# First attention in pairs of heads: suffix sums later, and from a high and a low part

## The chip, the cores and the metric

One core of a Trainium2 chip runs the whole program. Five engines work side by side, each through its own instructions in order: TensorE (PE: matmuls, and the loads of their stationary operand, PEld), VectorE (DVE), ScalarE (ACT), GpSimd (POOL), and SyncE (SP), whose queue issues the DMAs. They meet only at semaphores. The metric is the device time of the program in microseconds, the median of several runs.

## The reference, cut to what matters

The program computes one transformer block of one kind and then two of another, for 256 positions and a width of 1024, in float32. The change lies in the first block, in its "stick-breaking" attention (8 heads of 64 columns, queries in blocks of 128 positions):

```
z = q.k / sqrt(64)                                    for every query t and key s
log_not = where(s < t, log_sigmoid(-z), 0)
suffix = cumsum(log_not, over s, reverse) - log_not   # sum over the keys after s
a = where(s < t, exp(log_sigmoid(z) + suffix), 0)
o = a @ v                                             per head
```

Beside it the block computes `gates = sigmoid(h @ w_in[:, the last 3 * 1024 columns])`; the outputs of the attention, of a pooling branch and of a gating branch go through matrices of their own, are multiplied by these gates, and are added.

## The kernel before, in words

**Weights come in units.** Every large weight matrix is streamed from HBM in 153 units of 1 MB (128 partitions x 2048 numbers) through a ring of 4 slots (`raw`, `hi`, `lo`). float32 products are made from parts that TensorE takes in one pass: ACT copies a unit to the reduced type fp32r (`hi`, L356), DVE subtracts (`lo = raw - hi`, L367), and PE adds up three products per tile: high by high, low by high, high by low. `unit_x` (L466) does this with the activations as the stationary operand: for each of the two tiles of 128 positions (`for tt`), 4 k-tiles x 3 products of 512 columns, 12 matmuls a tile, 24 a unit. When its last matmul ends it raises `used`, ACT splits the unit that comes four units later (`act_step`), and DVE follows (`dve_step`). So a unit is split some three units ahead of its use, and for the weights alone neither ACT nor DVE has to hurry.

**The stage of the change.** The gates need 12 units, `s = 0..11`. The attention of the 8 heads is woven in between them, so that its chain through ACT and DVE runs beside matmuls of the units. In the code before, step `s` of PE is (block of TensorE, `for s in range(12)`):

- the 24 matmuls of gate unit `s`;
- `scores(s)`: z of head `s` into a PSUM bank, two matmuls (L1510, L1512) that use 64 of the 128 rows of the array;
- `suffix(s - 1)`: three matmuls with the constant matrices `tri` and `ones`, in float32, which add `log_not` up over the later keys;
- `values(s - 2)`: two matmuls with `vS`, which use 64 of the 128 output columns.

A float32 matmul stands in the trace as two instructions (two passes), an fp32r matmul as one.

ACT's step: the split of the unit (L356), `softplus(s)` (Abs, Exp, Ln: L1844, L1846, L1847), the exponential of head `s - 1` (L1881), in odd steps the high part of the attention's output (`o_split`, L1850) and the copy of a finished gate (L1858). DVE's step: the low part of the unit (L367), the argument of head `s - 1` (L2099: it adds the suffix sum from PSUM), `log_not(s)` (five instructions, L2081, L2083, L2087, L2089, L2091; `lnot_done` rises after the third), and in odd steps the low part of the output (L2107). In step 1 DVE also makes the norm of the gating branch (`gating_norm`, from L2060 to L2065). Only PSUM bank 6 holds a suffix sum, so `suffix(h)` waits until the argument of head `h - 1` has been read (`arg_done`).

After the gate units' step 9, PE makes the products of the pooling and the gating branch ("mixing", the 4 and 16 matmuls that read `wpd` and `wsT`), and in unit 10 goes on without attention work.

The order of work is what is written: no scheduler changes it. Each engine stands still at an instruction whose semaphore has not come, and everything behind it on that engine stands too.

## Time and profile before

| | us |
|---|---|
| median of 3 runs | 1027.43 |
| lowest, highest | 1025.7, 1028.62 |
| the profiled execution, its own time | 1026.62 |
| span of its trace | 1024.8 |
| PE busy | 1010.8 (99%) |
| DVE busy | 719.6 (70%) |
| ACT busy | 492.0 (48%) |
| stage of the change (scores of head 0 to gate unit 10) | 71.94 to 146.64 |

The program is one long row of matmuls, and an engine other than PE matters only where PE waits for it. The trace gives for each instruction its start and its duration. Matmuls overlap (a matmul of 512 columns is shown with 0.39 us, but the next starts 0.23 us later), so what a matmul costs is read from start to start; the same holds for ACT and DVE, whose instructions overlap by about 0.1 us.

### The profile page before, as it was taken

Reading aid. Unit: us, or ns where it says so; the run is one execution under the profiler, and the core shown is the slowest. Engines: PE = TensorE matmul, PEld = TensorE weight load, DVE = VectorE, ACT = ScalarE, POOL = GpSimd, SP = SyncE. Lnnn points to the kernel's source line nnn. Section 1 sums busy time; section 2 is a strip of 40 time slices with the busy share of each in tenths; the row PEclk is TensorE's granted clock in tenths of the full one; section 3 lists DMA queues with packets and bytes.
Section 4 is the critical chain, followed back from the end, with each engine's and each line's share of the span. In section 5 each row is a group of like instructions: output and inputs, shape, how many; then the busy total and the mean of one; then the engine's idle time right before and its main releaser. Section 6 shows DMA issues by size and latency. Waiting matters only on the chain.

```text
span 1024.8 us, 16248 instructions
## 1 busy us (share of the span) xinstructions
PE 1010.8 (99%) x6616; PEld 886.9 (87%) x6616; DVE 719.6 (70%) x882; ACT 492.0 (48%) x559; POOL 108.4 (11%) x83
## 2 busy tenths in 40 slices
PE   8999999999999999999999999999999999999998
PEld 8997778899999888986899999988886689999997
DVE  6869657987667787854887767677976776445664
ACT  6455564553444436432554343445556665343431
POOL 1031000000010000225001000010001301000000
PEclk9999999999999999999999999999999999999999
DMA  9984345749788784595639877786461536665641
GB/s 319 368 277 155 129 136 182 286 168 343 258 285 282 277 274 146 170 311 156 224 110 346 284 281 276 254 284 222 171 226 56 171 118 212 199 198 175 201 165 42
DMA packets 120031, 223.77 MB, mean 218 GB/s; under 512 B 6622, under 2 KB 21408, under 8 KB 119968
## 3 DMA queue, kind: packets, MB, share of 16 engines
q1 hardware_dynamic: 117584, 214.97, 61.6%
q0 software_dynamic: 2256, 7.88, 2.4%
q8 instruction: 45, 0.74, 0.3%
q14 instruction: 18, 0.15, 0.0%
q10 hardware_dynamic: 128, 0.03, 0.0%
HBM read 217.17 MB, written 1.05 MB: 213 GB/s over the span
## 4 chain that ended last, share of the span: by engine, by line
PE 88%; DVE 7%; issue 2%; ACT 1%; DMA 1%; POOL 1%; SPq 0%; DVEq 0%; ACTq 0%; POOLq 0%
PE ps L461 84%; DMA ada_raw<-in_ada_w 1%; PE ps L1120 1%; DVE lo L367 1%; PE ps L951 1%; ACT aS L1977 1%; DVE X L922 1%; PE ps L817 1%; POOL aS L2422 1%; DVE stat L2322 1%; PE ps L1510 0%; DMA X<-in_x 0%; DVE y_tmp L921 0%; ACT hi L356 0%; PE ps L1717 0%
## 5 line engine op out<-in xcount | busy, mean ns | idle before, releaser
L367 DVE TENSOR_TENSOR lo<-raw,hi 128x2048 fp32r<-128x2048 f32 x151 | 349.2, 2319 | 221.1 <-ACT hi L356 220.7
L356 ACT ACTIVATE hi<-raw 128x2048 fp32r<-128x2048 f32 x151 | 289.1, 1915 | 303.2 <-PE ps L461 274.8
L461 PE MATMUL ps<-hTh,hi 128*128 128x256 f32 x992 | 265.7, 286 | 1.1 <-DVE lo L367 0.6
L461 PE MATMUL ps<-hTh,lo 128*128 128x256 f32 x992 | 262.4, 283 | 0.0
L461 PE MATMUL ps<-hTl,hi 128*128 128x256 f32 x992 | 261.0, 283 | 0.0
L461 PEld LDWEIGHTS ps<-hTh,hi 128*128 128x128 f32 x992 | 182.1, 192 | 4.0 <-issue 2.8
L461 PEld LDWEIGHTS ps<-hTl,hi 128*128 128x128 f32 x992 | 181.7, 192 | 1.5 <-issue 1.2
L461 PEld LDWEIGHTS ps<-hTh,lo 128*128 128x128 f32 x992 | 182.2, 192 | 0.0
L461 PE MATMUL ps<-hi,hidh 128*128 128x512 f32 (+1 forms) x424 | 164.6, 388 | 0.0
L461 PE MATMUL ps<-hi,hidl 128*128 128x512 f32 (+1 forms) x424 | 163.5, 386 | 0.0
L461 PE MATMUL ps<-lo,hidh 128*128 128x512 f32 (+1 forms) x424 | 163.4, 385 | 0.0
L461 PE MATMUL ps<-hi,hTh 128*128 128x512 f32 (+1 forms) x328 | 128.0, 390 | 0.8 <-DVE hTl L2336 0.2
L461 PE MATMUL ps<-lo,hTh 128*128 128x512 f32 (+1 forms) x328 | 124.5, 380 | 0.0
L461 PE MATMUL ps<-hi,hTl 128*128 128x512 f32 (+1 forms) x328 | 122.0, 380 | 0.0
L1143 DVE SCALAR_TENSOR_TENSOR ada_acc<-ada_raw,cond,ada_acc 128x512 f32<-128x512 f32 x147 | 112.1, 762 | 7.1 <-DMA ada_raw<-in_ada_w 2.5
L1069 POOL TENSOR_TENSOR sqr<-relu 128x1024 f32<-128x1024 f32 x24 | 46.2, 1924 | 478.6 <-ACT relu L1037 478.6
L461 PEld LDWEIGHTS ps<-lo,hidh 128*128 128x128 f32 x424 | 79.6, 188 | 16.1
L461 PEld LDWEIGHTS ps<-hi,hidh 128*128 128x128 f32 x424 | 79.7, 188 | 15.9 <-DVE lo L367 0.5
L461 PEld LDWEIGHTS ps<-hi,hidl 128*128 128x128 f32 x424 | 79.7, 188 | 15.5 <-issue 0.5
L461 PEld LDWEIGHTS ps<-hi,hTh 128*128 128x128 f32 x328 | 61.7, 188 | 16.9 <-issue 3.8
L461 PEld LDWEIGHTS ps<-lo,hTh 128*128 128x128 f32 x328 | 61.7, 188 | 12.0
L461 PEld LDWEIGHTS ps<-hi,hTl 128*128 128x128 f32 x328 | 61.8, 188 | 11.0 <-issue 0.2
(248 smaller groups left out, 857.8 us busy)
## 6 DMA issues: line engine op xcount, KB each, us to landing
raw<-in_mlp_w SPq DMA_DIRECT2D x64, 1024.0 KB, 5.2
ada_raw<-in_ada_w SPq DMA_DIRECT2D x44, 1024.0 KB, 7.5
raw<-in_w_in SPq DMA_DIRECT2D x20, 1024.0 KB, 7.7
raw<-in_w_ff_in SPq DMA_DIRECT2D x16, 1024.0 KB, 5.4
raw<-in_w_ff_out SPq DMA_DIRECT2D x16, 1024.0 KB, 5.3
raw<-in_attn_w_qkv SPq DMA_DIRECT2D x12, 1024.0 KB, 6.1
raw<-in_conv_w_in SPq DMA_DIRECT2D x8, 1024.0 KB, 6.7
taps<-u_pad SPq DMA_DIRECT2D x64, 71.0 KB, 5.5
```

The source lines that it names most:

```text
L356: nc.scalar.activation(hi[:, slot], raw[:, slot], ACT.Copy).then_inc(hi_made, 1)
L367: nc.vector.tensor_tensor(lo[:, slot], raw[:, slot], hi[:, slot].bitcast(F32), ALU.subtract).then_inc(lo_made, 1)
L461: return nc.tensor.matmul(o, lhs, rhs, start=start, stop=False, skip_group_check=True)
L817: nc.tensor.matmul(ps[:, bank, 0:P], ident if by is None else by, ident if by is None else by, start=True, stop=True)
L922: nc.vector.tensor_tensor(x, x, y, ALU.add).then_inc((x_half, x_ver)[c], 1)
L951: nc.tensor.matmul(ps[:, 7], ones, ada_acc[:], start=True, stop=True).then_inc(ada_cols, 1)
L1069: nc.gpsimd.tensor_tensor(sqr[:], relu[:], relu[:], ALU.mult).then_inc(sq_done, 1)
L1120: last = nc.tensor.matmul(ps[:, bank, q:q + 1], acc[:, q * P:(q + 1) * P], ones[:, 0:1], start=True, stop=True)
L1143: ins = nc.vector.scalar_tensor_tensor(out=acc, in0=w, scalar=s, in1=acc, op0=ALU.mult, op1=ALU.add)
L1977: nc.scalar.activation(a, a, ACT.Exp, scale=SCALE, bias=s_col(k, 4 + j, 1), accum_out=s_col(k, 8 + j, 1)).then_inc(s_exp, 1)
L2322: link(dve, nc.vector.tensor_reduce(s_col(s, 2 * j, 2), aS[:, s % 4, :, c], AX.X, ALU.max))
L2422: nc.gpsimd.tensor_tensor(a, a, y, ALU.mult).then_inc(s_p, 1)
```

## The change

Four things change, all in the stage of the gate units:

- **Pairs.** `scores(k)` and `values(k)` now do heads `2k` and `2k+1` together, in even steps only. The two heads' matmuls stand next to each other, those of 256 columns first, then those of 128.
- **Later.** `suffix` of the even head comes at the end of the next, odd unit; `suffix` of the odd head in the middle of the unit after that (a new argument `middle` of `unit_x`, called between its two tiles); then `values(k)` and `scores(k + 1)` at that unit's end.
- **Two passes.** The suffix sum is made from an fp32r high part (`high(h)`, a copy on ACT) and an fp32r low part (a subtraction on DVE, the sixth instruction of `log_not`), with fp32r copies of the constants (`tri_r`, `ones_r`, made once on ACT): six fp32r matmuls instead of three float32 ones. The new semaphores are `hi_kept`, `lnot_lo` and `tri_kept`.
- **Order on ACT and DVE.** In even steps DVE does `log_not` of both heads, and ACT `softplus` of both, then `high` of both. The argument of the even head (`argument(s - 1)` in odd steps) stands behind that step's `dve_step`; the exponential of the even head stands behind `act_step`.

```diff
@@ -173,7 +173,10 @@
         sbt = ada_area("sbt", 4096, [P, 2, 3, 384])
+        sbt_r = ada_area("sbt_r", 4096, [P, 2, 3, 384], F32R)
         gt = ada_area("gt", 4096, [P, 3, 512])
+        tri_r = big("tri_r", 32768, [P, P], F32R)
+        ones_r = row_area("ones_r", 11648, [P, P], F32R)
...
@@ -460,7 +466,8 @@
-        def unit_x(pe, u, j, act_h, act_l, k0, outs, first, nk=4, cols=512, final=False, need=None, tail=None):
+        def unit_x(pe, u, j, act_h, act_l, k0, outs, first, nk=4, cols=512, final=False, need=None, tail=None,
+                   middle=lambda: None):
 
             slot = slot_of(u, j)
             pe.wait_ge(lo_made, u + 1)
@@ -484,6 +491,8 @@
                 return
             parts = UNIT // nk // cols
             for tt in range(TT):
+                if tt:
+                    middle()
                 for c in range(parts):
                     last = products(outs(tt, c), tt, slice(c * cols, (c + 1) * cols), first,
                                     need if tt == 0 and c == 0 else None)
@@ -1500,37 +1509,48 @@
                    True, nk=8, cols=SEQ)
             ada_sum(pe, 1)
 
-            def scores(h):
-                if h == 0:
+            def both(k):
+
+                return [(2 * k + i, slice(HD * i, HD * i + HD)) for i in range(2)]
+
+            def scores(k):
+                if k == 0:
                     pe.wait_ge(qkv_kept, 2)
-                if h >= 2:
-                    pe.wait_ge(arg_done, h - 1)
-                r = slice(HD * (h % 2), HD * (h % 2) + HD)
-                k = h // 2
-                nc.tensor.matmul(ps[:, 4 + h % 2, 0:SEQ], kT[r, k, 0:P], qT[r, k, :], start=True,
-                                 stop=False, skip_group_check=True)
-                nc.tensor.matmul(ps[:, 4 + h % 2, SEQ:384], kT[r, k, P:SEQ], qT[r, k, P:SEQ],
-                                 start=False, stop=False, skip_group_check=True).then_inc(z_done, 1)
+                else:
+                    pe.wait_ge(arg_done, 2 * k)
+                for h, r in both(k):
+                    nc.tensor.matmul(ps[:, 4 + h % 2, 0:SEQ], kT[r, k, 0:P], qT[r, k, :], start=True,
+                                     stop=False, skip_group_check=True)
+                for h, r in both(k):
+                    nc.tensor.matmul(ps[:, 4 + h % 2, SEQ:384], kT[r, k, P:SEQ], qT[r, k, P:SEQ],
+                                     start=False, stop=False, skip_group_check=True).then_inc(z_done, 1)
 
             def suffix(h):
 
-                pe.wait_ge(lnot_done, h + 1)
+                pe.wait_ge(hi_kept, h + 1)
                 if h >= 1:
                     pe.wait_ge(arg_done, h)
-                t = sbt[:, h % 2, 1]
-                mm(pe, ps[:, 6, 0:SEQ], tri, t[:, 0:SEQ], True)
-                mm(pe, ps[:, 6, P:SEQ], ones, t[:, SEQ:384])
-                mm(pe, ps[:, 6, SEQ:384], tri, t[:, SEQ:384]).then_inc(sfx_done, 1)
-
-            def values(h):
-                pe.wait_ge(a_done, h + 1)
-                if h >= 2 and h % 2 == 0:
-                    pe.wait_ge(o_lo, h // 2)
-                a = sbt[:, h % 2, 2]
-                r, at = slice(HD * (h % 2), HD * (h % 2) + HD), (h // 2 % 2) * SEQ
-                v = slice(h * HD, h * HD + HD)
-                mm(pe, ps[r, 7, at:at + SEQ], vS[:, 0, v], a[:, 0:SEQ], True)
-                mm(pe, ps[r, 7, at + P:at + SEQ], vS[:, 1, v], a[:, SEQ:384]).then_inc(av_done, 1)
+                if h == 0:
+                    pe.wait_ge(tri_kept, 2)
+                for i in range(2):
+                    t = sbt_r[:, h % 2, i]
+                    if i:
+                        pe.wait_ge(lnot_lo, h + 1)
+                    mm(pe, ps[:, 6, 0:SEQ], tri_r[:], t[:, 0:SEQ], i == 0)
+                    mm(pe, ps[:, 6, P:SEQ], ones_r[:], t[:, SEQ:384])
+                    last = mm(pe, ps[:, 6, SEQ:384], tri_r[:], t[:, SEQ:384])
+                last.then_inc(sfx_done, 1)
+
+            def values(k):
+                pe.wait_ge(a_done, 2 * k + 2)
+                if k:
+                    pe.wait_ge(o_lo, k)
+                at = (k % 2) * SEQ
+                for h, r in both(k):
+                    mm(pe, ps[r, 7, at:at + SEQ], vS[:, 0, h * HD:h * HD + HD], sbt[:, h % 2, 2, 0:SEQ], True)
+                for h, r in both(k):
+                    mm(pe, ps[r, 7, at + P:at + SEQ], vS[:, 1, h * HD:h * HD + HD],
+                       sbt[:, h % 2, 2, SEQ:384]).then_inc(av_done, 1)
 
             for s in range(12):
                 g = s // 2
@@ -1542,14 +1562,15 @@
                     pe.wait_ge(gelu_done, 2)
                 elif s % 2 == 0:
                     pe.wait_ge(gate_kept, g - 1)
+                odd_head = s % 2 == 0 and 2 <= s <= SB_HEADS
                 unit_x(pe, U_GATE + s, None, hTh, hTl, 4 * (s % 2), lambda tt, c: ps[:, bank + tt],
-                       s % 2 == 0)
-                if s < SB_HEADS:
-                    scores(s)
-                if 1 <= s < SB_HEADS + 1:
+                       s % 2 == 0, middle=(lambda: suffix(s - 1)) if odd_head else lambda: None)
+                if s % 2 and s < SB_HEADS:
                     suffix(s - 1)
-                if 2 <= s < SB_HEADS + 2:
-                    values(s - 2)
+                if odd_head:
+                    values(s // 2 - 1)
+                if s % 2 == 0 and s < SB_HEADS:
+                    scores(s // 2)
                 if s == 9:
 
                     pe.wait_ge(pool_in, 1)
@@ -1833,6 +1854,9 @@
             gelu(ps[:, 2], gv[:].rearrange("p t n -> p (t n)"))
             nc.scalar.preload_act_table_set("natural_log_exp_and_others")
 
+            nc.scalar.activation(tri_r[:], tri, ACT.Copy).then_inc(tri_kept, 1)
+            nc.scalar.activation(ones_r[:], ones, ACT.Copy).then_inc(tri_kept, 1)
+
             def softplus(h):
 
                 act.wait_ge(z_done, h + 1)
@@ -1845,6 +1869,15 @@
                 act.wait_ge(abs_done, h + 1)
                 link_act(act, nc.scalar.activation(t, t, ACT.Exp, scale=-1.0))
                 nc.scalar.activation(t, t, ACT.Ln, bias=1.0).then_inc(soft_done, 1)
+
+            def weights(h):
+                act.wait_ge(arg_done, h + 1)
+                a = sbt[:, h % 2, 2]
+                nc.scalar.activation(a, a, ACT.Exp).then_inc(a_done, 1)
+
+            def high(h):
+                act.wait_ge(lnot_done, h + 1)
+                nc.scalar.activation(sbt_r[:, h % 2, 0], sbt[:, h % 2, 1], ACT.Copy).then_inc(hi_kept, 1)
 
             def o_split(k, bank, cols):
                 nc.scalar.activation(hidh[:, k], ps[:, bank, cols], ACT.Copy).then_inc(o_hi, 1)
@@ -1871,18 +1904,21 @@
                         gate_sigmoid(g)
                 if s == 11:
                     gate_from_bank(5, ACT.Sigmoid)
+                if s % 2 == 0 and 2 <= s <= SB_HEADS:
+                    weights(s - 1)
                 act_step(act, U_GATE + s)
-                if s < SB_HEADS:
+                if s % 2 == 0 and s < SB_HEADS:
                     softplus(s)
-                if 1 <= s < SB_HEADS + 1:
-                    h = s - 1
-                    act.wait_ge(arg_done, h + 1)
-                    a = sbt[:, h % 2, 2]
-                    nc.scalar.activation(a, a, ACT.Exp).then_inc(a_done, 1)
-                if s % 2 and s >= 3 and s < SB_HEADS + 2:
-                    k = (s - 3) // 2
+                    softplus(s + 1)
+                    high(s)
+                if s % 2 == 0 and 2 <= s <= SB_HEADS:
+                    k = s // 2 - 1
                     act.wait_ge(av_done, 2 * k + 2)
                     o_split(k, 7, slice((k % 2) * SEQ, (k % 2 + 1) * SEQ))
+                if s % 2 == 0 and s < SB_HEADS:
+                    high(s + 1)
+                if s % 2 and s < SB_HEADS:
+                    weights(s - 1)
                 if s == 9:
                     nc.scalar.preload_act_table_set(SIGMOIDS)
                     gate_from_bank(4, ACT.Sigmoid)
@@ -2089,20 +2125,28 @@
                 link(dve, nc.vector.scalar_tensor_tensor(out=t3, in0=z, scalar=SCALE, in1=t2,
                                                          op0=ALU.mult, op1=ALU.add))
                 link(dve, nc.vector.tensor_tensor(diagonals(t3), diagonals(t3), n2, ALU.add))
+                dve.wait_ge(hi_kept, h + 1)
+                nc.vector.tensor_tensor(sbt_r[:, h % 2, 1], t2, sbt_r[:, h % 2, 0].bitcast(F32),
+                                        ALU.subtract).then_inc(lnot_lo, 1)
+
+            def argument(h):
+                dve.wait_ge(sfx_done, h + 1)
+                t3 = sbt[:, h % 2, 2]
+                nc.vector.tensor_tensor(t3, t3, ps[:, 6, 0:384], ALU.add).then_inc(arg_done, 1)
 
             for s in range(12):
+                if s % 2 == 0 and 2 <= s <= SB_HEADS:
+                    argument(s - 1)
                 dve_step(dve, U_GATE + s)
-                if 1 <= s < SB_HEADS + 1:
-                    h = s - 1
-                    dve.wait_ge(sfx_done, h + 1)
-                    t3 = sbt[:, h % 2, 2]
-                    nc.vector.tensor_tensor(t3, t3, ps[:, 6, 0:384], ALU.add).then_inc(arg_done, 1)
-                if s < SB_HEADS:
+                if s % 2 and s < SB_HEADS:
+                    argument(s - 1)
+                if s % 2 == 0 and s < SB_HEADS:
                     log_not(s)
+                    log_not(s + 1)
                 if s == 1:
                     gating_norm()
-                if s % 2 and s >= 3 and s < SB_HEADS + 2:
-                    k = (s - 3) // 2
+                if s % 2 == 0 and 2 <= s <= SB_HEADS:
+                    k = s // 2 - 1
                     dve.wait_ge(o_hi, k + 1)
                     nc.vector.tensor_tensor(hidl[:, k], ps[:, 7, (k % 2) * SEQ:(k % 2 + 1) * SEQ],
                                             hidh[:, k].bitcast(F32), ALU.subtract).then_inc(o_lo, 1)
```

How the instructions stand on PE, before, at the end of a gate unit (its last and the next unit's first matmul are `lo,hTh` and `hi,hTh`; `sbt,cst` is a suffix sum, `sbt,vS` are the values, `qT,kT` the scores; here and below each row is an instruction of the program, with its output's shape):

```order
L461 MATMUL ps<-lo,hTh 128x512
L1510 MATMUL ps<-qT,kT 128x256
L1512 MATMUL ps<-qT,kT 128x128
L461 MATMUL ps<-sbt,cst 128x256
L461 MATMUL ps<-sbt,cst 128x128 x2
L461 MATMUL ps<-sbt,vS 64x256
L461 MATMUL ps<-sbt,vS 64x128
L461 MATMUL ps<-hi,hTh 128x512
```

On PE in the changed kernel, in the middle of an even unit (s = 4), the suffix sum of the odd head:

```order
L467 MATMUL ps<-lo,hTh 128x512
L467 MATMUL ps<-sbt_r,tri_r 128x256
L467 MATMUL ps<-sbt_r,ones_r 128x128
L467 MATMUL ps<-sbt_r,tri_r 128x128
L467 MATMUL ps<-sbt_r,tri_r 128x256
L467 MATMUL ps<-sbt_r,ones_r 128x128
L467 MATMUL ps<-sbt_r,tri_r 128x128
L467 MATMUL ps<-hi,hTh 128x512
```

and at the end of the same unit the values of one pair and the scores of the next:

```order
L467 MATMUL ps<-lo,hTh 128x512
L467 MATMUL ps<-sbt,vS 64x256 x2
L467 MATMUL ps<-sbt,vS 64x128 x2
L1522 MATMUL ps<-qT,kT 128x256 x2
L1525 MATMUL ps<-qT,kT 128x128 x2
L467 MATMUL ps<-hi,hTh 128x512
```

Each group of scores and values now holds two heads, and the suffix sum has left the unit's end for the middle in every other unit.

DVE before, over one unit step (the low part of a unit, the argument of the head before, then `log_not` of this head):

```order
L367 TENSOR_TENSOR lo<-raw,hi 128x2048
L2099 TENSOR_TENSOR sbt<-sbt,ps 128x384
L2081 TENSOR_SCALAR sbt<-ps 128x384
L2083 SCALAR_TENSOR_TENSOR sbt<-sbt 128x384
L2087 TENSOR_TENSOR sbt<-sbt,cst 128x2x128
L2089 SCALAR_TENSOR_TENSOR sbt<-ps,sbt 128x384
L2091 TENSOR_TENSOR sbt<-sbt,cst 128x2x128
```

DVE in the changed kernel, from `log_not` of a pair's odd head (L2117 to L2129) to the arguments (L2135):

```order
L2117 TENSOR_SCALAR sbt<-ps 128x384
L2119 SCALAR_TENSOR_TENSOR sbt<-sbt 128x384
L2123 TENSOR_TENSOR sbt<-sbt,cst 128x2x128
L2125 SCALAR_TENSOR_TENSOR sbt<-ps,sbt 128x384
L2127 TENSOR_TENSOR sbt<-sbt,cst 128x2x128
L2129 TENSOR_TENSOR sbt_r<-sbt,sbt_r 128x384
L2151 TENSOR_TENSOR hidl<-ps,hidh 128x256
L373 TENSOR_TENSOR lo<-raw,hi 128x2048
L2135 TENSOR_TENSOR sbt<-sbt,ps 128x384 x2
```

Between two arguments there stood one unit's low part and one `log_not`; now both arguments come together, behind two `log_not` and the low part of the odd unit.

ACT in the changed kernel, from the second `softplus` of a pair (L1868, L1870, L1871) through `high` (L1880), `o_split` (L1883), `high`, the odd unit's split (L362), the exponential of the even head (L1876), the gate's copy (L1891) and the exponential of the odd head, to the next even unit's split:

```order
L1868 ACTIVATE sbt<-ps 128x384
L1870 ACTIVATE sbt<-sbt 128x384
L1871 ACTIVATE sbt<-sbt 128x384
L1880 ACTIVATE sbt_r<-sbt 128x384
L1883 ACTIVATE hidh<-ps 128x256
L1880 ACTIVATE sbt_r<-sbt 128x384
L362 ACTIVATE hi<-raw 128x2048
L1876 ACTIVATE sbt<-sbt 128x384
L1891 ACTIVATE gate<-ps 128x1024
L1876 ACTIVATE sbt<-sbt 128x384
L362 ACTIVATE hi<-raw 128x2048
```

The odd unit's split now stands behind `high` of the odd head, which waits for DVE.

## Rows read from the trace of the kernel before

**Rows 1.** The page: span, busy time by engine, and TensorE's granted clock.
```profile
span 1024.8 us, 16248 instructions
...
PE 1010.8 (99%) x6616; PEld 886.9 (87%) x6616; DVE 719.6 (70%) x882; ACT 492.0 (48%) x559; POOL 108.4 (11%) x83
...
PEclk9999999999999999999999999999999999999999
```
**Rows 2.** Waits of PE: us in total, times, longest.
```profile
PE ps L1760 <- POOL aS L2422: 4.3, 4, 1.3
```
**Rows 3.** Windows: length, busy us of PE, PEld, DVE, ACT, POOL; clock.
```profile
102.70:119.54 16.84, 16.84 (x78) 12.92 (x77) 10.81 (x15) 8.93 (x12) 0.00 (x0) 1.00 0.37 126
...
136.38:146.64 10.26, 10.26 (x59) 7.63 (x58) 3.63 (x3) 5.24 (x5) 0.00 (x0) 1.00 0.37 118
```
**Rows 4.** Timeline of PE after a gate unit: start, us, engine, line.
```profile
94.28 0.70 PE L1510 MATMUL ps<-qT,kT 64*128 64x256 f32 x2
...
95.12 1.14 PE L461 MATMUL ps<-sbt,cst 128*128 128x256 f32 x6
...
96.20 0.86 PE L461 MATMUL ps<-sbt,vS 128*64 128x256 f32 x4
...
96.99 0.50 PE L461 MATMUL ps<-hi,hTh 128*128 128x512 f32 x1
...
97.33 0.40 PE L461 MATMUL ps<-hi,hTl 128*128 128x512 f32 x1
```
**Rows 5.** Timeline of PE in the second attention, where heads stand in pairs.
```profile
802.80 0.88 PE L461 MATMUL ps<-aT,Vs 128*64 128x256 f32 x8
...
803.61 0.93 PE L461 MATMUL ps<-kT,qT 64*128 64x128 f32 x8
```
**Rows 6.** Timeline of PE, fp32r matmuls of 256 columns.
```profile
219.89 0.64 PE L461 MATMUL ps<-hTh,hi 128*128 128x256 f32 x4
220.37 0.64 PE L461 MATMUL ps<-hTh,lo 128*128 128x256 f32 x4
```
**Rows 7.** Timeline of ACT in the same gate step.
```profile
94.39 1.91 ACT L356 ACTIVATE hi<-raw 128x2048 fp32r<-128x2048 f32 x1 [0.45 <-PE ps L461]
96.20 0.47 ACT L1844 ACTIVATE sbt<-ps 128x384 f32<-128x384 f32 x1
...
99.19 0.53 ACT L1881 ACTIVATE sbt<-sbt 128x384 f32<-128x384 f32 x1 [1.40 <-DVE sbt L2099]
99.62 0.37 ACT L1850 ACTIVATE hidh<-ps 128x256 fp32r<-128x256 f32 x1
```
**Rows 8.** Timeline of DVE in the same gate step.
```profile
96.40 2.29 DVE L367 TENSOR_TENSOR lo<-raw,hi 128x2048 fp32r<-128x2048 f32 x1 [0.33 <-ACT hi L356]
98.61 0.55 DVE L2099 TENSOR_TENSOR sbt<-sbt,ps 128x384 f32<-128x384 f32 x1
99.07 0.55 DVE L2081 TENSOR_SCALAR sbt<-ps 128x384 f32<-128x384 f32 x1
...
100.82 0.56 DVE L2089 SCALAR_TENSOR_TENSOR sbt<-ps,sbt 128x384 f32<-128x384 f32 x1
...
101.87 0.42 DVE L2107 TENSOR_TENSOR hidl<-ps,hidh 128x256 fp32r<-128x256 f32 x1
```
**Rows 9.** Timeline of DVE in the first two gate steps.
```profile
73.99 2.71 DVE L367 TENSOR_TENSOR lo<-raw,hi 128x2048 fp32r<-128x2048 f32 x1 [3.96 <-ACT hi L356]
...
80.61 2.29 DVE L367 TENSOR_TENSOR lo<-raw,hi 128x2048 fp32r<-128x2048 f32 x1
...
86.09 0.42 DVE L2060 SCALAR_TENSOR_TENSOR gv_sq<-gv 128x256 f32<-128x256 f32 x1
...
90.62 2.29 DVE L367 TENSOR_TENSOR lo<-raw,hi 128x2048 fp32r<-128x2048 f32 x1
```
**Rows 10.** Timeline of PE at the end of the stage.
```profile
144.51 1.13 PE L461 MATMUL ps<-pp,wpd 128*128 128x256 f32 x4
...
146.64 0.50 PE L461 MATMUL ps<-hi,hTh 128*128 128x512 f32 x1
```

More of the change, by code:

```diff
@@ L299, in build_kernel @@
         lnot_done = sem("lnot_done")
+        hi_kept = sem("hi_kept")
+        lnot_lo = sem("lnot_lo")
+        tri_kept = sem("tri_kept")
         sfx_done = sem("sfx_done")
```

## The prediction, made before the changed kernel ran

> **What bounds the kernel now.** First the page: PE is busy for 1010.8 of 1024.8 us, and its granted clock stands at the upper level (2.4 GHz) in all 40 slices [rows 1]. Then PE's waits: the longest group sums to 4.3 us in the whole run, none over 1.3 us, and it belongs to the second attention [rows 2]. Then windows over the stage of the change: from one even step's scores to the next PE is busy for all of 16.84 us, while DVE has 10.81 and ACT 8.93 us of work [rows 3]. So today the stage costs exactly what PE has to do, and the chain through ACT and DVE is hidden. Two questions follow: how much PE work goes, and whether the new chain through ACT and DVE still fits beside the rest. I answer the second with the timelines of the three engines, start to start, since that is what an instruction costs its engine.
>
> **PE's own work.** From the timeline [rows 4]: scores of one head 94.28 to 95.12 = 0.84 us, suffix sum 1.08, values 0.79; together 2.71 a step, and a unit takes 8.42 (half of 16.84) - 2.71 = 5.71, so 2.85 a half. The second attention already runs heads in pairs: both heads' values take 802.80 to 803.61 = 0.81 us, both heads' scores last 0.93 with their tail [rows 5]. So matmuls on different halves of the array overlap there, and I take 0.85 for a pair's scores and 0.81 + 0.15 = 0.96 for its values. The 0.15 is for leaving the unit's stream: the first matmul after such a group costs 0.34 instead of 0.23 [rows 4]. The two-pass suffix sum is six fp32r matmuls, two of 256 columns and four of 128. Those of 256 cost 0.12 each (0.48 for four) [rows 6]. For 128 columns in fp32r there is no row. Bounds: half of 0.12, which gives 0.48 for the six; or as dear as a 512-column one, 0.24 each, which gives 1.2. I take 0.12 each, the nearest row: 0.72, and 0.87 with the switch. Saved in all: scores 4 x (1.68 - 0.85) = 3.3, values 4 x (1.58 - 0.96) = 2.5, suffix sums 8 x (1.08 - 0.87) = 1.7, together 7.5 us.
>
> [...]
>
> **The new chain.** What matters is where the argument of a pair's even head stands. The odd head's suffix sum wants to start on PE in the middle of unit 2k+2, and it waits for `arg_done` of the even head, because both use PSUM bank 6. On DVE this argument now stands behind both `log_not` and behind the low part of the odd unit, which waits for ACT's split, which stands on ACT behind `high` of the odd head, which waits for DVE's `log_not` of that head. I follow it from the moment `used` of unit 2k rises:
>
> - to ACT's split 0.11 (94.28 to 94.39) [rows 4, 7]; to DVE's low part 2.01 (94.39 to 96.40); to the next on DVE 2.21 [rows 7, 8];
> - `log_not` of the even head 2.80 (99.07 to 101.87) and the new subtraction 0.46 (as L2099, the same size: 98.61 to 99.07): 3.26;
> - `log_not` of the odd head up to its third result 1.75 (99.07 to 100.82);
> - `high` of the odd head 0.45. There is no row; the nearest are a copy of 256 columns with 0.37 and an Exp of 384 with 0.53, 0.43 start to start [rows 7], so between 0.35 and 0.55;
> - ACT's split and DVE's low part of the odd unit 2.01 + 2.21; the argument, until another engine can use it, 0.58 (98.61 to 99.19).
>
> That is 14.59 us. PE in the same time has values 0.96, scores 0.85, unit 5.70, suffix sum 0.87 and half a unit 2.85: 11.23. So **PE stands still for 3.4 us** at the odd head's suffix sum, in each pair. Behind it on PE stands everything: the second half of the unit, values, scores, the next unit. After the stall come suffix sum 0.87 and half a unit 2.85, and `used` rises again. Cycle: 14.59 + 3.72 = 18.31 us, against 16.84 now: +1.47 for a pair, three times (`used` of unit 2 to that of unit 8): **+4.4**.
>
> Two of the savings lie off this chain. Scores and values of a pair run while ACT and DVE do the split and low part of unit 2k (4.2 us), and the even head's suffix sum runs before the stall; whatever they cost, PE only waits longer or shorter. The low pass of the even head's sum wants its data at 0.11 + 2.01 + 2.21 + 3.26 = 7.6 us, and PE comes there after 7.5: a tie.
>
> **The first pair** costs more, since today step 0 and 1 have little attention work, and `gating_norm` is in it. ACT's split for unit 0 feeds DVE at 73.99, and that low part with `log_not(0)` lasts until 80.61 [rows 9]; it stays so. Then: subtraction to 81.07, `log_not(1)` to 82.82, `high` 83.27, split 85.28, low part 87.49, argument usable at 88.07, where PE has been waiting since about 84.4. DVE goes on with `gating_norm`, 4.53 us (86.09 to 90.62) [rows 9], from 87.95 to 92.48, and only then comes the odd head's argument, usable at 93.06. ACT's exponential (0.43) ends at 93.49, and there ACT begins the split for unit 2. Today that is at 94.39 - 8.42 = 85.97. So **+7.5**. PE waits about 3.6 us before the odd suffix sum and about 1.8 us before the first values.
>
> **The end.** From `used` of unit 8, today at 136.38, to unit 10 at 146.64 are 10.26 us [rows 3, 10]. Then: values 0.96, unit 5.70, mixing 2.13 (144.51 to 146.64): 8.79. **-1.5**. The two constant copies on ACT lie in its idle time before the first scores, two short instructions.
>
> Sum: 7.5 + 4.4 - 1.5 = +10.4 us. The profiled execution has 1026.62 us, so 1037.0; the median shown is 0.8 higher, which gives 1037.8. I forecast **1037.5**. Nothing gives it back later: PE is full behind this stage too, and all its waits longest by group come to a few us in 1024.8. Own range: 128-column matmuls at either bound -1 to +2 (four odd suffix sums on the chain), `high` and the subtraction +-0.6, hand-overs some +-1: 1034.5 to 1041.
>
> **Rivals.**
> 1. *The stall also costs clock* (slower still). Rows: the clock stays at the upper level throughout, and the longest wait in front of PE is 1.3 us [rows 1, 2], so nothing here shows what follows a stall of 3.4 us. Against it: PE works over 80% of each pair. Price: after a stall, suffix sum and half unit (3.7 us) are on the chain; at the lower level (1.2 GHz) they would take twice as long, at most +3.7 for each of four stalls. With half of that, +7: 1044.
> The Trainium skill (TensorE: Matmul & The Clock Gate, "Why this matters for your kernels") warns that idle gaps between bursts of matmuls put the clock back to its lower level; the trace has no such gap to agree or disagree with.
> 2. *Only the first pair pays.* If the hand-overs overlap more than my rows say and the pair's chain is 1.5 us shorter, later pairs break even at 16.84, and +7.5 - 1.5 leaves 1033.5. For it: the sum has nine terms, each read from a step in which an engine was partly idle. Against it: the same terms, added up in today's order, give today's starts to 0.3 us.
> 3. *PE stays the bound* (the other side: faster). Here the argument of the even head would be there when PE reaches the middle of unit 2k+2; from then on only PE's work counts, 7.5 us less: 1019.5. The point of decision is 11.23 us after `used`; my chain comes 3.4 us later, and no price of a pair's matmuls changes that, only ACT and DVE. The order of the instructions is fixed in the code, so I give it little.
> 4. *Nothing changes within what can be told*: stalls and savings would cancel, which needs a first pair of +3 instead of +7.5.
>
> **How the numbers follow.** Forecast 0.67, clock 0.15, only the first pair 0.11, PE-bound 0.04, no change 0.03. The last two are all that is not slower; 0.3% (3 us) is about what a measurement of this kernel can tell from no change. So faster 0.04, same 0.03, slower 0.93. The range reaches from just under rival 2 to near rival 1: 1032 to 1043.
>
> **What would show it.** In the profile after: PE no longer full in 80 to 140 us, with four waits of some 3 us in front of an fp32r matmul on `sbt_r`, released by DVE's argument (L2135); a wait of about 2 us before the first values; 18.3 us from a pair's scores to the next; the six fp32r matmuls in about 0.8 us; a pair's values and scores in 1.8 us; PEclk unchanged. I am wrong if PE has no waits there, if the wait is for the low part or the exponential instead, if the pairs follow each other in under 17 us, or if PEclk falls behind the stalls.

## The result, and the profile after

The changed kernel takes **1040.8 us** (median of 4 runs, 1038.33 to 1041.29) against 1026.57 us for the kernel before on the same chip: ratio **1.0125 [1.011 to 1.0139]**, slower by 14 us between the medians. (The ratio on record weighs all runs and is not the quotient of the medians; by it the loss is 12.8 us.) The forecast was 1037.5 us with a range of 1032 to 1043. The profiled execution has 1041.29 us, of them 1039.5 in the span. Runs of one kernel differ by some 2 us with their mean granted clock (beside warm_fill, the kernel before has a median of 1026.3 us in its 16 runs at 1.000 and of 1028.1 us in its 5 at 0.998), so a difference under 2 us is read from the ratio's interval and the trace, not from two medians.

The page of the changed kernel: PE and TensorE's clock in the 40 slices (26 us each).

```profile
PE 1010.0 (97%) x6616; PEld 886.3 (85%) x6616; DVE 724.8 (70%) x890; ACT 495.8 (48%) x569; POOL 108.5 (10%) x83
...
PE   8997789999999999999999999999999899999998
...
PEclk9998989999999999999999999999999999999999
```

Compare [rows 1]: PE's busy time is nearly the same although its matmuls in the stage should need some 7 us less. In slices 4 to 6 (78 to 156 us) PE is no longer full, and the clock has two dips, in slices 4 and 6. Both belong together, as the next views show. PE's waits in the changed kernel (total, times, longest):

```profile
PE ps L467 <- DVE sbt L2135: 10.8, 4, 3.5
...
PE ps L467 <- ACT sbt L1876: 1.8, 1, 1.8
PE ps L467 <- ACT sbt_r L1880: 1.3, 1, 1.3
...
PE ps L467 <- DVE sbt_r L2129: 0.8, 1, 0.8
```

Before, the largest group in the whole run was one of 4.3 us in another stage [rows 2]. L2135 is DVE's argument, L1876 the exponential of the even head, L1880 and L2129 the high and the low part. The timeline of PE puts them in their places (start, us, in brackets the wait ahead):

```profile
87.95 0.36 PE L467 MATMUL ps<-sbt_r,tri_r 128*128 128x256 f32 x1 [2.01 <-DVE sbt L2135]
...
93.41 0.87 PE L467 MATMUL ps<-sbt,vS 128*64 128x256 f32 x8 [1.80 <-ACT sbt L1876]
...
107.65 0.36 PE L467 MATMUL ps<-sbt_r,tri_r 128*128 128x256 f32 x1 [1.83 <-DVE sbt L2135]
...
109.51 0.63 PE L467 MATMUL ps<-lo,hTh 128*128 128x512 f32 x1
109.93 0.63 PE L467 MATMUL ps<-hi,hTh 128*128 128x512 f32 x1
...
112.06 0.40 PE L467 MATMUL ps<-hi,hTh 128*128 128x512 f32 x1
112.30 0.39 PE L467 MATMUL ps<-hi,hTl 128*128 128x512 f32 x1
...
112.85 0.87 PE L467 MATMUL ps<-sbt,vS 128*64 128x256 f32 x8
...
127.35 0.36 PE L467 MATMUL ps<-sbt_r,tri_r 128*128 128x256 f32 x1 [3.48 <-DVE sbt L2135]
...
132.54 0.87 PE L467 MATMUL ps<-sbt,vS 128*64 128x256 f32 x8
```

The reader is to see two things. Each odd head's suffix sum waits for the argument of the even head, as forecast. And behind that wait the unit's matmuls start 0.42 us apart (109.51, 109.93) and only later 0.24 (112.06, 112.30). The windows of PE say why (length, busy us, clock, DMA share, GB/s):

```profile
104.00:108.00 4.00, 2.17 (x12) 1.53 (x11) 3.14 (x4) 1.17 (x3) 0.00 (x0) 1.00 0.00 0
108.00:112.00 4.00, 4.00 (x15) 3.32 (x14) 0.56 (x1) 1.50 (x3) 0.00 (x0) 0.57 0.77 266
124.00:128.00 4.00, 0.65 (x6) 0.68 (x6) 2.85 (x3) 1.18 (x3) 0.00 (x0) 1.00 0.06 8
128.00:132.00 4.00, 4.00 (x14) 3.14 (x13) 0.56 (x1) 1.20 (x2) 0.00 (x0) 0.58 0.68 254
...
148.00:152.00 4.00, 4.00 (x12) 3.23 (x12) 0.55 (x1) 0.90 (x2) 0.00 (x0) 0.50 0.67 254
```

(Busy times stand as in [rows 3], all five engines.) After these stretches, in which PE waits for 1.8 to 3.5 us, the granted clock is 0.50 to 0.58: for most of 4 us the lower level, 1.2 GHz. PE is fully busy there and does little over half as much. That is why its busy time did not fall. A window over a whole pair, as in [rows 3]:

```profile
112.85:132.54 19.69, 16.21 (x77) 12.60 (x76) 11.93 (x17) 9.86 (x14) 0.00 (x0) 0.91 0.30 107
```

19.69 us, where a pair took 16.84 before.

### The profile page after: what moved, and what is told of

Its sections match the earlier page's. It is cut to its first block, busy times and chain, and to the rows that moved or that the text cites. A ratio compares the mean times of both kernels' runs of the same rounds, so it can differ in the third digit from the quotient of the medians.

```text
span 1039.5 us, 16268 instructions
## 1 busy us (share of the span) xinstructions
PE 1010.0 (97%) x6616; PEld 886.3 (85%) x6616; DVE 724.8 (70%) x890; ACT 495.8 (48%) x569; POOL 108.5 (10%) x83
## 4 chain that ended last, share of the span: by engine, by line
PE 82%; DVE 10%; ACT 3%; issue 3%; DMA 1%; POOL 1%; SPq 0%; DVEq 0%; ACTq 0%; POOLq 0%
PE ps L467 79%; DVE lo L373 1%; ACT hi L362 1%; DMA ada_raw<-in_ada_w 1%; PE ps L1129 1%; PE ps L960 1%; ACT aS L2013 1%; DVE X L931 1%; PE ps L826 1%; POOL aS L2466 1%; DVE stat L2366 0%; DVE sbt L2119 0%; DVE sbt L2117 0%; DMA X<-in_x 0%; DVE y_tmp L930 0%
## 5 line engine op out<-in xcount | busy, mean ns | idle before, releaser
L362 ACT ACTIVATE hi<-raw 128x2048 fp32r<-128x2048 f32 x151 | 288.9, 1914 | 297.8 <-PE ps L467 270.1
L467 PE MATMUL ps<-hi,hTh 128*128 128x512 f32 (+1 forms) x328 | 131.2, 400 | 0.8 <-DVE hTl L1304 0.2
L467 PE MATMUL ps<-lo,hTh 128*128 128x512 f32 (+1 forms) x328 | 127.0, 387 | 0.0
L467 PE MATMUL ps<-hi,hTl 128*128 128x512 f32 (+1 forms) x328 | 124.5, 388 | 0.0
```

The lines of the kernel that those rows point to most:

```text
L362: nc.scalar.activation(hi[:, slot], raw[:, slot], ACT.Copy).then_inc(hi_made, 1)
L467: return nc.tensor.matmul(o, lhs, rhs, start=start, stop=False, skip_group_check=True)
```

## The experiments

Each is timed beside the kernel before; the ratio, with its interval, weighs all runs of both. Where two variants are compared, their medians can come from different chips.

**The clock behind the stalls.** PE does unused float32 matmuls in the time in which it would wait: if the clock is what goes beyond the forecast, the time falls though work is added. The long form, warm_fill:

```diff
+            def fill(n, bank):
+                for _ in range(n):
+                    nc.tensor.matmul(ps[:, bank, 0:P], ident, ident, start=True, stop=True)
             def suffix(h):
+                if h == 0:
+                    fill(8, 3)
+                if h % 2:
+                    fill(20, chunk_bank((h + 1) // 2) + 1)
```

> The changed kernel with unused matmuls in front of the waits: 20 float32 matmuls of 128x128 (about 2.6 us) before each odd head's suffix sum, into the PSUM bank that the unit's second tile is about to fill, and 8 before the first suffix sum. Waits, order and data are unchanged; the output is the same. Theory: of the 14.2 us lost, about 9 are the stalls themselves and about 5 the lower clock that follows them. Then the granted clock stays near 1.00 here, a pair takes 18.3 us instead of 19.7, and the time is 1035 to 1037 us. Rival A: the slow stretches behind the stalls have another cause than the idle time; then the matmuls there stay at 0.43 us and the time at 1041. Rival B: the fillers run past the moment when the data comes and cost more than they give: above 1041.

Measured: 1036.87 us, ratio 1.0104 [1.0089, 1.012]. As expected in time, and the clock is 1.00 through the stage. But 20 such matmuls took 4.4 us (they show as 40 instructions of 0.11 us) and in later pairs ran past the argument. So a shorter form, fill_short, with 4 and 14 matmuls in place of 8 and 20:

> The changed kernel with fewer unused matmuls in front of the waits: 14 before each odd suffix sum and 4 before the first, instead of 20 and 8. A float32 matmul is two instructions of 0.11 us each, so 20 of them took 4.4 us, not the 2.6 that I had reckoned, and in that trace PE was still at them 0.8 us after the argument could be used (125.82 + 0.7, suffix sum at 127.27). Theory: with 3.1 us of filling they fit in the stall; the three later pairs lose their 0.8 us, and the clock is still held up. So 1036.9 - 3 x 0.8 = 1034.5, and the whole loss by the clock in the changed kernel is about 6 us. Rival: the wait that is left open lets the clock fall again: over 1037.

Measured: 1035.57 us, ratio 1.008 [1.0067, 1.0094], 1 us above what I expected. Its PE timeline and windows:

```profile
107.82 0.36 PE L467 MATMUL ps<-sbt_r,tri_r 128*128 128x256 f32 x1 [0.27 <-DVE sbt L2144]
...
111.41 0.87 PE L467 MATMUL ps<-sbt,vS 128*64 128x256 f32 x8
...
125.89 0.36 PE L467 MATMUL ps<-sbt_r,tri_r 128*128 128x256 f32 x1 [0.34 <-DVE sbt L2144]
...
129.50 0.87 PE L467 MATMUL ps<-sbt,vS 128*64 128x256 f32 x8
```

```profile
112.00:130.00 18.00, 17.66 (x108) 14.65 (x106) 11.92 (x17) 9.77 (x15) 0.00 (x0) 1.00 0.35 117
```

The clock stays at the upper level, PE still waits for the same instruction (0.27 and 0.34 us), and a pair takes 18.09 us (111.41 to 129.50), near the 18.31 of the forecast. From the wait's end to the values are 3.59 us, in the changed kernel 5.20 (107.65 to 112.85). So the lower clock costs 1040.8 - 1035.57 = **5.2 us** (4.6 by the ratios; 5.8 in the two profiled executions, from the first scores to the last values: 71.85 to 153.18 against 72.03 to 147.60). This shows it, since the kernel differs in nothing but added work.

**The order on DVE.** The forecast's chain says that the argument stands too late on DVE. arg_first moves one call:

```diff
-                dve_step(dve, U_GATE + s)
                 if s % 2 and s < SB_HEADS:
                     argument(s - 1)
+                dve_step(dve, U_GATE + s)
```

> The changed kernel with one line moved: in odd steps DVE makes the even head's argument before the low part of the odd unit, not behind it. Theory: the stall at the odd head's suffix sum is made by the order on DVE and ACT (argument behind the low part, that behind ACT's split, that behind the high part of the odd head). Without it the argument is there 11.9 us after the unit's last use instead of 14.6, PE comes at 11.2, and a pair takes 15.6 us instead of 19.7; the first pair still waits for the gating norm before the odd head's argument. So +7 in the first pair, 3 x -1.3, -1.8 at the end, against the kernel before: 1028 to 1030 us, and hardly a stretch at the lower clock after the first pair. Rival: what PE waits for is not this order but the length of two log_not plus the new parts; then the stalls stay over 2 us and the time over 1036.

Measured: 1027.8 us, ratio 1.0012 [1.0003, 1.0021]. One call takes back 13 of the 14 us. The waits for the argument are now 3 times at most 0.8 us. Those of the first suffix sum stay (1.3 and 0.8 us), and one long wait is left, before the first values:

```profile
92.78 0.87 PE L467 MATMUL ps<-sbt,vS 128*64 128x256 f32 x8 [3.47 <-ACT sbt L1876]
```

```profile
80.00:90.00 10.00, 8.47 (x35) 0.83 0.25 77
90.00:100.00 10.00, 7.22 (x40) 1.00 0.36 119
```

(The second fence has length, PE's busy time, clock, DMA share, GB/s.) Behind this wait of 3.47 us the clock does not fall in the profiled execution, though it fell behind the two short waits at 80 us. So a long wait is not always followed by the lower clock.

**The norm of the gate values** stands on DVE between the two arguments of the first pair. gating_late puts it in step 8 (and lets the copy of the fifth gate on ACT wait for it):

```diff
+                if s == SB_HEADS:
+                    gating_norm()
                 dve_step(dve, U_GATE + s)
...
-                if s == 1:
-                    gating_norm()
```

> The changed kernel with the gating branch's norm moved on DVE from step 1 to step 8, behind the last argument (ACT's copy of the fifth gate waits for it, since they share memory). Theory: in the first pair the norm, 4.5 us, stands between the two arguments, so the first values wait 1.8 us for it and the next split on ACT starts late. Without it 1.6 us go, and some of the lower clock behind that wait: 1037.5 to 1039.5. Rival: the first pair is as long for another reason and the norm only fills time that DVE has: 1040.8, no change.

Measured: **1042.82 us**, ratio 1.0162 [1.0148, 1.0176]: slower than the changed kernel (the intervals of the two ratios do not overlap), where I had expected a gain or, as the rival, no change. In the profiled executions the difference is only 0.3 us (1041.63 against 1041.29). PE in its first pair, and the window behind:

```profile
87.69 0.55 PE L467 MATMUL ps<-sbt_r,tri_r 128*128 128x256 f32 x1 [3.43 <-DVE sbt L2136]
...
89.96 0.63 PE L467 MATMUL ps<-lo,hTh 128*128 128x512 f32 x1
90.38 0.63 PE L467 MATMUL ps<-hi,hTh 128*128 128x512 f32 x1
...
94.11 0.87 PE L467 MATMUL ps<-sbt,vS 128*64 128x256 f32 x8
```

```profile
88.00:92.00 4.00, 4.00 (x13) 0.50 0.77 262
```

The wait before the first values is gone, but what is behind the 3.43 us stall now runs at the lower level: 6.42 us from suffix sum to values (87.69 to 94.11) instead of the 3.6 of fill_short's later pairs. It is so behind the first three stalls; behind the fourth, of 3.48 us before 149.94, the clock is 1.00 and the values come 3.60 us later. In the changed kernel the first pair's stall is 2.01 us and 88:92 has a clock of 1.00; the slow stretches there fell at about 81 to 84 and 94 to 98 us, where PE has a wait ahead of it anyway. Two runs test this reading: the same move with PE kept busy, in the long form and in the short one.

> The changed kernel with the gating norm in step 8 and the unused matmuls in front of the waits. The norm's move alone gave 1042.8, against 1038.5 expected: in its trace the wait before the first values was gone, but the half unit behind the first stall of 3.4 us ran at the lower clock, where before it had run at the upper. Theory: the gain of 1.6 us is real and was more than taken back because the slow stretch now falls on the chain. With the clock held up it must come out: 1.6 us under the kernel with the filling matmuls alone (1036.9): 1034.8 to 1035.8. Rival: the move costs something by itself (the fifth gate's copy that now waits, the norm in step 8): then it is at or above 1036.9 here too.

Measured: 1036.07 us, ratio 1.0091 [1.0074, 1.0107]. The sign is right, the gain over warm_fill is 0.8 us and not 1.6, with overlapping intervals: the long filler overruns the wait and hides part of it.

> The same short filling with the gating norm in step 8. With the long filling the norm's move gave 0.8 us where 1.6 was expected; there the matmuls of the first pair overran too, so that the first stall ended later and hid part of the gain. Theory: here the full 1.6 us show against the kernel with the short filling alone: 1032.5 to 1033.5. Rival: the norm's move is worth only 0.8 us whatever the filling: 1033.7 or more.

Measured: 1033.89 us, ratio 1.0066 [1.0052, 1.008]. Against fill_short, on the same chip and with no run of one among those of the other, that is -1.7 us; the time is above the expected 1033.5 only because fill_short's is. So the same move is worth -1.7 us at a steady clock and +2.0 without: the clock decides its sign. The +2.0 is the looser number: in the profiled executions, first scores to last values, the move gives -1.6 us with the filler and +0.6 without, so the clock's term is 2 to 4 us.

**Both moves** (arg_first and gating_late), both_moves:

> The changed kernel with both moves: the even head's argument before the low part, the gating norm in step 8. Theory: now the savings on PE come out (7.5 us by the estimate from paired and fp32r matmuls), less about 2 us of waits at the first suffix sum and under 1 us at each odd one: 1022 to 1025 us, faster than the kernel before. Rival: the pairs and the two-pass sum save little on PE, and only the stalls are gone: 1026 to 1028. Second rival: another wait appears in place of the one removed (for the exponential of the odd head, or the low pass): above 1028.

Measured: 1024.07 us, ratio 0.9979 [0.997, 0.9988]. With the stalls short the clock keeps its upper level in the stage of the profiled execution (a slow stretch lies far behind it, at 380 to 400 us with 0.91), and the kernel is 2.3 us faster than the one before. Its PE in a later pair:

```profile
111.31 0.28 PE L467 MATMUL ps<-sbt_r,tri_r 128*128 128x256 f32 x1
...
112.10 0.45 PE L467 MATMUL ps<-hi,hTh 128*128 128x512 f32 x1
...
115.87 0.36 PE L467 MATMUL ps<-sbt_r,tri_r 128*128 128x256 f32 x1 [0.82 <-DVE sbt L2136]
```

The wait is down to 0.82 us, and the even head's six matmuls take 0.79 (111.31 to 112.10), since the low part comes late. Ahead of the argument DVE still has the output's low part; both_out_late puts it behind, in the odd steps:

```diff
-                if s % 2 == 0 and 2 <= s <= SB_HEADS:
-                    k = s // 2 - 1
+                if s % 2 and 3 <= s <= SB_HEADS + 1:
+                    k = (s - 3) // 2
                     dve.wait_ge(o_hi, k + 1)
```

> Both moves, and the low part of a pair's output (0.34 us on DVE) behind the even head's argument, not before it. Theory: with both moves PE still waits 0.8 us for the even head's argument in each of the last three pairs, and every piece of DVE's work ahead of it is on the chain: 3 x 0.34 = 1.0 us less than with both moves (1024.1): 1023.1. Rival: the chain is already bound elsewhere (the low pass, the exponential of the odd head), and nothing comes: 1024.1.

Measured: 1022.82 us, ratio 0.9963 [0.9949, 0.9978]. The waits for the argument sum to 1.9 us instead of 2.9, as expected; the intervals of the two ratios overlap, so the gain of 1.3 us between the medians is not clear of the noise.

**The two passes by themselves.** Three kernels. pairs_float32 is the changed kernel with nothing moved, but float32 suffix sums and neither high nor low part:

```diff
-                for i in range(2):
-                    t = sbt_r[:, h % 2, i]
-                    if i:
-                        pe.wait_ge(lnot_lo, h + 1)
-                    mm(pe, ps[:, 6, 0:SEQ], tri_r[:], t[:, 0:SEQ], i == 0)
...
+                t = sbt[:, h % 2, 1]
+                mm(pe, ps[:, 6, 0:SEQ], tri, t[:, 0:SEQ], True)
...
-                nc.vector.tensor_tensor(sbt_r[:, h % 2, 1], t2, sbt_r[:, h % 2, 0].bitcast(F32),
-                                        ALU.subtract).then_inc(lnot_lo, 1)
```

> The changed kernel with one part undone: float32 suffix sums as before, no high and low parts; pairs, places and the order of arguments as in the change, nothing moved. Theory: the order is what stalls PE, the two-pass parts only lengthen it. Without them ACT's split of the odd unit no longer waits for DVE, the argument of the even head can be used 13.1 us after the unit's last use (2.0 + 2.2 + 5.6 + 0.3 + 2.2 + 0.6 and 0.1), PE comes there after 11.7: stalls of 1.4 us instead of 3.4, 17.2 us a pair, about +6 us in the first pair. Stage +5 to +7 us over the kernel before, and little or no lower clock: 1032 to 1034. Rival A: the two-pass parts alone make the stall; then there is none here and the time is 1023 to 1027. Rival B: they have nothing to do with it: 1039 or more.

Measured: 1032.35 us, ratio 1.0046 [1.0032, 1.0059] (the kernel before has 1028.29 beside it). The four waits for the argument are 3.2 us and three times 2.0, where I had expected 1.4 in a pair. Two pairs take 16.8 and 16.9 us, not 17.2; the last takes 18.5, because the clock still gives way behind the first and the fourth wait (88 to 96 us and 136 to 144 us), against what I expected:

```profile
88.00:96.00 8.00, 7.99 (x38) 5.93 (x37) 4.93 (x13) 4.40 (x7) 0.00 (x0) 0.81 0.29 109
...
136.00:144.00 8.00, 5.96 (x22) 4.61 (x20) 3.22 (x3) 1.96 (x3) 0.00 (x0) 0.79 0.43 131
```

Without the two passes' extra instructions on ACT and DVE 8 of the 14 us are gone, the part of them that is clock included. two_pass_only is the opposite: the kernel before with the six fp32r matmuls, `high` at the end of ACT's step, and the norm in step 8.

```diff
+                if s < SB_HEADS:
+                    high(s)
...
-                if s == 1:
+                if s == SB_HEADS:
                     gating_norm()
```

> The kernel before with the two-pass suffix sums alone (single heads, the order of before; ACT makes the high part at the end of its step; the gating norm in step 8, since in step 1 it would stand before data that PE waits for). Theory: 8 x 0.45 = 3.6 us less work on PE, of which some 1.5 us are lost at the first suffix sum, which now waits for both parts; single heads have 8.4 us of PE work a step against 6 us on DVE, so there are no stalls elsewhere: 1024 to 1025. Rival: the parts come too late in each step and PE waits: 1026.5 or more.

Measured: 1026.44 us, ratio 0.9996 [0.9987, 1.0005]: no gain, where I expected 1.5 to 2.5 us. PE around one suffix sum:

```profile
87.75 0.39 PE L467 MATMUL ps<-sbt_r,tri_r 128*128 128x256 f32 x1
...
88.58 0.86 PE L467 MATMUL ps<-sbt,vS 128*64 128x256 f32 x4
```

The six take 0.83 us straight behind the scores, not 0.63. A step is 8.12 us (88.58, 96.70, 104.83), 0.3 shorter than before, and not 0.45. But the step with the first suffix sum is 1.4 us longer (scores at 78.14 and 86.90, before 78.47 and 85.86), as it waits 0.44 and 0.85 us for its parts. From the first scores to the mixing 0.6 us are left (71.61 to 143.56, before 71.94 to 144.51), less than these medians can tell. both_float32 is both_moves with float32 suffix sums:

> Both moves, with the suffix sums in float32 as in the kernel before: no high and low part on ACT and DVE, three float32 matmuls a head. This takes the two-pass sum out of the change and leaves pairs and order. Theory: PE has 0.45 us more a head (1.08 against the 0.63 measured), but ACT and DVE have less in front of the argument (0.46 and 0.45 us a head), so that the waits of 0.8 us and part of those at the first suffix sum go: about even, 1023.5 to 1025. Rival: the two-pass sum is the larger part of what is gained; then 1026 to 1028 here.

Measured: 1022.79 us, ratio **0.9951 [0.9936, 0.9966]**, better than I expected, with both_out_late the best here and ahead of both kernels. Its pair is 14.7 us (102.63, 117.34), with the argument in time. In both_moves it is 15.44. So with the pairs in place the two passes bring nothing on PE that their late data does not take back.

Its stage (first scores to gate unit 10) is 6.2 us shorter than before, the kernel only 3.7. Where the rest goes: PE in both_float32 in two later stretches, then the kernel before.

```profile
380.00:400.00 20.00, 18.28 (x117) 1.00 0.45 153
450.00:480.00 30.00, 27.81 (x394) 1.00 0.78 210
```

```profile
380.00:400.00 20.00, 19.06 (x100) 1.00 0.76 259
450.00:480.00 30.00, 30.00 (x380) 1.00 0.85 245
```

PE is idle 0.8 and 2.2 us more in them, the second time for a result of DVE (L2255, 2.2 us in two waits). That is about as much as is missing (2.5 us). What makes DVE late there I have not tested. It need not be so in every run: two of its six took 1020.26 and 1020.64 us, some 6 us less than the kernel before.

## Why the prediction came out right, step by step

- **The stall's mechanism: right.** The four waits are for the instruction named, at the place named. From ACT's split of unit 2k to the odd suffix sum the chain gave 14.59 - 0.11 = 14.48 us. ACT's splits and the last link on DVE in the changed kernel:

```profile
93.27 1.90 ACT L362 ACTIVATE hi<-raw 128x2048 fp32r<-128x2048 f32 x1
...
102.38 0.53 ACT L1880 ACTIVATE sbt_r<-sbt 128x384 fp32r<-128x384 f32 x1 [2.49 <-DVEq L821]
102.81 1.90 ACT L362 ACTIVATE hi<-raw 128x2048 fp32r<-128x2048 f32 x1
...
112.96 1.91 ACT L362 ACTIVATE hi<-raw 128x2048 fp32r<-128x2048 f32 x1 [3.06 <-PE ps L467]
```

```profile
104.75 2.29 DVE L373 TENSOR_TENSOR lo<-raw,hi 128x2048 fp32r<-128x2048 f32 x1 [0.37 <-ACT hi L362]
106.96 0.55 DVE L2135 TENSOR_TENSOR sbt<-sbt,ps 128x384 f32<-128x384 f32 x1
```

  93.27 to PE's start at 107.65 is 14.38 us, and in the next pair 112.96 to 127.35 is 14.39. `high` took 0.43 (102.38 to 102.81), forecast 0.45.
- **The size of the stall: 3.4 us forecast, 3.48 us** in the third and fourth pair (the fourth at 147.05). In the second it is 1.83, because PE came there later: the slow stretch at 94 to 98 us lay ahead of the wait and was absorbed by it.
- **The first pair: +7.5 forecast.** ACT's split for unit 2 starts at 93.27 instead of 85.97: +7.3. But the wait before the odd suffix sum was 2.0 us, not 3.6. I had missed two waits in the first suffix sum, 1.3 us for the high and 0.8 for the low part; with a slow stretch behind them (below) they made PE late for the stall, and since DVE set the time they cost nothing.

```profile
80.00:84.00 4.00, 3.15 (x11) 0.60 0.19 75
```

- **The later pairs: +4.4 forecast, +9.5 measured. This is the step that failed**: "behind it suffix sum 0.87 and half a unit 2.85", 3.72 us. Measured are 5.20, 5.19 and 6.13 (to 153.18), 1.5 to 2.4 us more in each, because PE runs at the lower clock right behind the stall. I had this as rival 1, with 0.15 and a price of +7 for four stalls. Three stalls paid, and fill_short puts the price at 5.2. The forecast's own mechanism without that gives 18.31 a pair where fill_short shows 18.09. The chance was too small: the kernel before had no wait over 1.3 us, so its steady clock told nothing of what follows 3.4 us.
  The Trainium skill (TensorE: Matmul & The Clock Gate, "Why this matters for your kernels") warns that idle gaps between bursts of matmuls put the clock back; weighed against a trace without a gap it got too little weight. Here the trace agrees: 0.50 in 148:152, behind a wait of 3.48 us. It does not always: behind the 3.47 us of arg_first the clock stays at 1.00.
- **The end: -1.5 forecast, -1.8 measured** (from ACT's split at unit 8's last use to gate unit 10: 153.28 to 161.63, 8.35 us; before 136.49 to 146.64, 10.15).
- **PE's savings off the chain: right.** A pair's values take 0.80 us and its scores 0.86 (112.85, 113.65, 114.5), 1.8 forecast. The six fp32r matmuls take 0.63 inside a unit, where the row of 256 columns had led me to 0.72: those of 128 start 0.06 to 0.12 us after each other. In the later pairs the even head's six take 0.81 (120.11 to 120.92), since the low part comes late. None of it moved the time, as said; arg_first shows that it counts once the argument comes early.
- **The sum:** +7.3 + 9.5 - 1.8 = +15.0 at unit 10, and 14.7 between the two profiled executions. Nothing was given back later, as forecast.
- **Rivals 2 to 4** (only the first pair pays, PE-bound, no change) fell with the pairs at 18 us and more. "PEclk unchanged" was wrong, and I had named it as a sign against me: the direction and most of the size came from the forecast's own chain. Part of the closeness is luck: that chain without the clock measures 1035.57 (fill_short), 1.9 us less than the 1037.5 forecast, of which 0.9 is the base (median 1026.57 now, 1027.43 then) and the rest small terms; the clock, put at nothing, adds 5.2. The two errors have opposite signs, and 3.3 us are left.

The Trainium skill (FP8 and Floating Point Precision, TensorE Precision Notes) has a true float32 product at four passes and names no count for the reduced form. If that is one pass, two of them are half of float32's 1.08 us, 0.54 as an estimate from the page. Measured are 0.63 within a unit, half way between this 0.54 and my 0.72, and 0.83 behind the scores; it decided nothing.

## What to carry to other kernels

When work is moved on PE, write down for every value that PE will wait for what stands ahead of its producer on the producer's engine: here one call on DVE, behind a step that itself waited for another engine, turned 7.5 us of expected savings into a loss of 14, and moving that call took back 13. A stall of some 3 us on PE costs its length and can cost the slower clock behind it, unless another wait follows that swallows it; whether the clock falls could not be told here from the length of the wait. Try unused matmuls in the stall to measure that part by itself, and price a removed short wait with it, since joining two waits into one long one can lose time. And a saving counts only with the data in time: cheaper matmuls that need two more steps on other engines gained nothing here.

## What the runs showed of the hardware

- The granted clock fell to its lower level (matmuls 0.42 us apart instead of 0.23) behind five of seven waits of 3.4 to 3.5 us: both in the changed kernel and three of four in gating_late, but not the one in arg_first. It also fell in the first pair behind waits of 1.3 and 0.8 us close together (0.60 in 80:84), while behind the same two waits in gating_late and both_moves it stayed at 1.00. What decides this the runs leave open. A slow stretch lasted from some 3 us (108 to 111) to some 6 (146 to 152).
- Unused 128-column float32 matmuls in the waits kept it up in all four kernels that had them (1.00 throughout the stage), at 0.11 us for each of the two instructions that one shows as.
- A slow stretch costs nothing where a wait on another engine follows: the second pair's stall was 1.83 us instead of 3.48.
- The matmuls of two heads on different halves of the array ran side by side: values of one head 0.79 us before, of two 0.80; scores 0.84 and 0.86.
